# Routing weights from two fp32r products, x kept in DRAM meanwhile, steps from tile 40

## What is computed

```python
def peer_ffn(h, w_q, sub_keys, peer_u, peer_v):       # 8 heads, 128 x 128 experts, top 16
    q = einsum('td,de->te', xb, w_q)
    s = einsum('thpk,pnk->thpn', q, sub_keys)         # scores of two halves of a key
    s_top, i_top = top_k(s, 16)
    g_top, pos = top_k(sums of the two halves, 16)    # 16 experts (i, j) per head and token
    g = softmax(g_top)
    act = gelu(einsum('thk,td->thk', peer_u[expert], xb))
    return einsum('thk,thkd->td', g * act, peer_v[expert])
```

## Time and profile before

| | |
|---|---|
| median of 3 runs | 2617.55 us |
| the profiled execution's own time | 2617.07 us |
| its span (first to last instruction) | 2615.2 us |
| TensorE (PE) busy | 2562.4 us, 98% |
| VectorE (DVE) busy | 2056.7 us, 79% |
| ScalarE (ACT) busy | 1549.1 us, 59% |
| mean granted TensorE clock | 0.992 |

### The profile page before, as it was taken

One profiled execution on the slowest core, in us unless ns is written; L12 is line 12 of the kernel. 1 busy time (PEld: TensorE's weight loads), 2 busy tenths in 40 slices (PEclk: granted clock), 3 DMA queues, 4 the chain that ended last, 5 costly groups with the idle time before them and its releaser, 6 DMA issues.

```text
span 2615.2 us, 46815 instructions
## 1 busy us (share of the span) xinstructions
PE 2562.4 (98%) x16116; PEld 2305.1 (88%) x16116; DVE 2056.7 (79%) x4002; ACT 1549.1 (59%) x2687; POOL 321.2 (12%) x182
## 2 busy tenths in 40 slices
PE   6999999999999999999999999999999999999998
PEld 5779989999888888989989999888888888889887
DVE  6778978889888887679878888766666886688866
ACT  3455577766666666555577666665554555564543
POOL 3107700000000002717500000000000001100000
PEclk8999999999999999999999999999999999999999
DMA  6845574444788885424564444555556356643554
GB/s 228 285 151 173 187 248 151 145 141 148 259 291 289 292 281 163 170 95 166 203 225 146 146 145 146 201 193 201 192 192 207 106 166 203 202 149 131 182 192 137
DMA packets 138427, 492.42 MB, mean 188 GB/s; under 512 B 18704, under 2 KB 18792, under 8 KB 137984
## 3 DMA queue, kind: packets, MB, share of 16 engines
q1 hardware_dynamic: 135600, 481.90, 53.8%
q0 software_dynamic: 2640, 8.02, 1.0%
HBM read 488.79 MB, written 1.07 MB: 187 GB/s over the span
## 4 chain that ended last, share of the span: by engine, by line
PE 90%; DVE 6%; ACT 2%; DMA 1%; issue 1%; POOL 0%; SPq 0%; DVEq 0%; ACTq 0%
PE ps L236 70%; PE ps L242 7%; PE ps L1491 4%; PE ps L243 4%; DMA weight_ring<-in_stream 1%; DVE weight_split L271 1%; PE ps L2659 1%; PE ps L1455 1%; DVE hT_split L496 1%; ACT weight_split L262 0%; DVE hT_split L495 0%; DVE stat L621 0%; PE ps L450 0%; DVE x L618 0%; POOL weight_split L271 0%
## 5 line engine op out<-in xcount | busy, mean ns | idle before, releaser
L262 ACT ACTIVATE weight_split<-weight_ring 128x1024 fp32r<-128x1024 f32 x800 | 848.7, 1062 | 228.4 <-DMA weight_ring<-in_stream 139.2
L271 DVE TENSOR_TENSOR weight_split<-weight_ring,weight_split 128x1024 fp32r<-128x1024 f32 x684 | 829.5, 1221 | 135.1 <-ACT weight_split L262 131.7
L236 PE MATMUL ps<-hT_split,weight_split 128*128 128x256 f32 x7224 | 923.5, 286 | 4.2 <-POOL weight_split L271 2.3
L236 PE MATMUL ps<-weight_split,hidden_split 128*128 128x512 f32 x3948 | 911.3, 390 | 0.0
L236 PEld LDWEIGHTS ps<-hT_split,weight_split 128*128 128x128 f32 x7224 | 885.7, 193 | 10.8 <-issue 7.1
L236 PEld LDWEIGHTS ps<-weight_split,hidden_split 128*128 128x128 f32 x3948 | 736.2, 188 | 156.1 <-issue 1.0
L271 POOL TENSOR_TENSOR weight_split<-weight_ring,weight_split 128x1024 fp32r<-128x1024 f32 x116 | 282.2, 2438 | 123.0 <-ACT weight_split L262 122.8
L242 PE MATMUL ps<-hT_split,weight_split 128*128 128x512 f32 x816 | 291.4, 398 | 0.5 <-DVE hT_split L496 0.5
L1586 ACT ACTIVATE hidden_split<-arena 128x256 fp32r<-128x256 f32 (+1 forms) x256 | 175.4, 685 | 178.5 <-PE ps L236 178.1
L1758 DVE TENSOR_TENSOR hidden_split<-arena,hidden_split 128x256 fp32r<-128x256 f32 x256 | 163.8, 640 | 90.5 <-ACT hidden_split L1586 90.1
L243 PE MATMUL ps<-hT_split,weight_split 128*128 128x256 f32 x816 | 229.0, 281 | 0.0
(11 more groups left out here) (377 smaller groups left out, 1979.5 us busy)
## 6 DMA issues: line engine op xcount, KB each, us to landing
weight_ring<-in_stream SPq DMA_DIRECT2D x912, 512.0 KB, 3.4
arena<-gate_rows SPq DMA_DIRECT2D x3, 512.0 KB, 5.4
x<-in_x SPq DMA_DIRECT2D x1, 1024.0 KB, 5.1
arena<-mlstm_m_rows POOLq DMA_DIRECT2D x1, 1024.0 KB, 6.1
arena<-in_ln_mix_g POOLq DMA_DIRECT2D x2, 512.0 KB, 5.4
arena<-in_ln_mix_b POOLq DMA_DIRECT2D x2, 512.0 KB, 7.9
arena<-in_ln_ffn_g POOLq DMA_DIRECT2D x2, 512.0 KB, 4.8
arena<-in_ln_ffn_b POOLq DMA_DIRECT2D x2, 512.0 KB, 6.7
```

The source lines that it names most:

```text
L236: mm = pe.matmul(out_, stationary(s_part), moving(m_part), start=start and n == 0, stop=stop and n == 2, skip_group_check=True)
L262: act.activation(wsplit[:, n % SPLITS, HIGH, :], ring[:, slot(POS[n]), :], ACT.Copy).then_inc(high_ready, 1)
L271: eng.tensor_tensor(w[:, REST, :], ring[:, slot(POS[n]), :], w[:, HIGH, :].bitcast(fp32), ALU.subtract).then_inc(split_ready, 1)
```

## The change

- An expert's weight w is parted into its rounding to fp32r, h, and the ratio (w - h) / h (`weight_parts`, VectorE, once per layer ahead of the first step). `places_i` now holds h, in fp32r. A token takes two fp32r matmuls in place of one fp32 matmul, with the same stationary matrix: one with the ones of the second place, one with the ratio in their place. Their sum is w.
- VectorE makes the ones for all 4 tokens of a step (`places_j`), first in its pass; ScalarE multiplies them with the ratio, 4 activations with a scale per partition (`places_low`), which wait for VectorE. The distance and the Relu go.
- `pr_ohi` and the ratio's matrices lie where x is; x is written to DRAM at the start of the up stage and read back in the down stage, both by SyncE's queue. The places of the ones have two buffers, not three.
- STEP_AT: 64 steps over tiles 40 to 124, at a distance of 1.2 tiles at first and 1.5 at the end. Wide tiles are 30 to 39, no more 30 to 50; a step ahead of tile 51 weighs and keeps in the early part of `acts` too.

```diff
-("down0", "ssa", 56), ...  ("down1", "s", 64), ...
+("down0", "ssa", 8), ("down0_more", "ssa", 48), ...  ("down1", "s", 16), ("down1_more", "s", 48), ...
-STEP_AT = [j for j in range(52, 125) if (j - 52) % 8 != 7]
+STEP_AT = [40 + (1512 * q + 27 * q * q // 10) // 1260 for q in range(64)]
+WIDE_FROM = 30
...
+        with nc.sbuf_tensor("step_parts", [128, 2, 2, 4, 128], fp32r) as step_parts:
+            pass
         x = sbuf("x", [128, TB, D])
...
-        pr_ohi = edge_b.rearrange("p (n a i) -> p n a i", n=2, a=STEP)
-        pr_ohj = hidden[:].rearrange("p n a t -> p (n a t)").rearrange("p (n a i) -> p n a i", n=3, a=STEP)
+        pr_ohi, pr_ohj_low = step_parts[:, 0], step_parts[:, 1]
+        pr_ohj = hidden[:, 0:2].rearrange("p n a t -> p (n a t)").rearrange("p (n a i) -> p n a i", n=2, a=STEP)
+        pr_low, pr_high = hidden[:, 2, 0, :], hidden[:, 2, 1, :]
...
         def wide(j):
-            return 30 <= j < 51
+            return WIDE_FROM <= j < FIRST_STEP
...
                 for a in range(STEP):
-                    mm = pe.matmul(ps[:, q % 3, 128 * a:128 * a + 128], pr_ohi[:, q % 2, a, :], pr_ohj[:, q % 3, a, :].bitcast(fp32),
-                                   start=True, stop=True)
+                    weights = ps[:, q % 3, 128 * a:128 * a + 128]
+                    pe.matmul(weights, pr_ohi[:, q % 2, a, :], pr_ohj[:, q % 2, a, :], start=True, stop=False, skip_group_check=True)
+                    mm = pe.matmul(weights, pr_ohi[:, q % 2, a, :], pr_ohj_low[:, q % 2, a, :], start=False, stop=True, skip_group_check=True)
...
+            def places_low(q):
+                if q == 0:
+                    act.wait_ge(pr_low_r, l + 1)
+                    act.wait_ge(x_moved, 16 * (2 * l + 1))
+                act.wait_ge(pr_ohj_dve, STEPS * l + q + 1)
+                if q >= 2:
+                    act.wait_ge(pr_built, STEPS * l + q - 1)
+                for a in range(STEP):
+                    t = STEP * q + a
+                    step = act.activation(pr_ohj_low[:, q % 2, a, :], pr_ohj[:, q % 2, a, :].bitcast(fp32), ACT.Copy, scale=pr_low.bitcast(fp32)[:, t:t + 1])
+                step.then_inc(pr_ohj_act, 1)
...
             for j in range(128):
+                if j + 1 in STEP_AT:
+                    places_low(with_step(j + 1))
                 if j - 1 in STEP_AT:
                     keep(with_step(j - 1))
-                if j + 1 in STEP_AT:
-                    places_j(with_step(j + 1))
...
+            def weight_parts():
+                dve.wait_ge(pr_cols_out, 2 * (l + 1))
+                whole, high, inverse = pr_cols[:, 2, :], pr_high.bitcast(fp32), edge_b[:, 0:T]
+                after_dve(dve.tensor_copy(pr_high, whole))
+                after_dve(dve.tensor_tensor(whole, whole, high, ALU.subtract), dve.tensor_scalar(inverse, high, 1e-30, None, ALU.max))
+                after_dve(dve.reciprocal(inverse, inverse))
+                dve.tensor_tensor(pr_low, inverse, whole, ALU.mult).then_inc(pr_low_r, 1)
+                dve.wait_ge(pr_low_r, l + 1)
+                dve.wait_ge(x_moved, 16 * (2 * l + 1))
...
             for j in range(HEAD, 129):
+                if j + 1 in STEP_AT:
+                    if with_step(j + 1) == 0:
+                        weight_parts()
+                    places_j(with_step(j + 1))
                 if j - 1 in STEP_AT:
                     weigh(with_step(j - 1))
...
-                if j + 1 in STEP_AT:
-                    places_j(with_step(j + 1))
...
+            dve.wait_ge(x_moved, 16 * (2 * l + 2))
             residual_dve(2 * l + 1, 3 if l else 1, edge_b, td + 128, HY_T if l else SB_T, None if l else 2)
...
+            def x_out(l):
+                eng.wait_ge(x_ready, 2 * l + 1)
+                eng.dma_start(x_kept, x[:]).then_inc(x_moved, 16)
+
+            def x_back(l):
+                eng.wait_ge(pr_built, STEPS * (l + 1))
+                eng.dma_start(x[:], x_kept).then_inc(x_moved, 16)
+
+            beside = {"up0": lambda: x_out(0), "down0_more": lambda: x_back(0), "up1": lambda: x_out(1), "down1_more": lambda: x_back(1),
```

More of the change, by code:

```diff
@@ L1595, in keep @@
                 act.wait_ge(pr_routed, STEPS * l + q + 1)
[L1596 to L1600, removed]
-                for a in range(ACT_J):
-                    step = act.activation(pr_ohj[:, q % 3, a, :], iota[:], ACT.Abs, scale=-1.0, bias=pr_cols[:, 1, STEP * q + a:STEP * q + a + 1])
-                step.then_inc(pr_distance, 1)
-                act.wait_ge(pr_distance, STEPS * l + q + 1)
-                near = pr_ohj[:, q % 3, 0:ACT_J]
-                act.activation(near, near.bitcast(fp32), ACT.Relu, scale=-1.0, bias=1.0).then_inc(pr_ohj_act, 1)
+                at, tokens = STEP_AT[q], slice(STEP * q, STEP * q + STEP)
+                if at < EARLY:
+                    act.activation(acts_early[:, tokens, at:], step_weights(q)[:, :, at:EARLY], ACT.Copy)
+                late = max(at, EARLY)
+                act.activation(acts_late[:, tokens, late - EARLY:], step_weights(q)[:, :, late:], ACT.Copy).then_inc(pr_kept, 1)
+            def places_low(q):
[9 more added lines that the diff above has]
+                step.then_inc(pr_ohj_act, 1)
             def exps():
@@ L1739, in places_i, with places_j @@
             def places_i(q):
+                for a in range(STEP):
+                    t = STEP * q + a
+                    step = dve.tensor_scalar(pr_ohi[:, q % 2, a, :], iota[:], pr_cols[:, 0, t:t + 1], pr_high.bitcast(fp32)[:, t:t + 1], ALU.is_equal, ALU.mult)
+                step.then_inc(pr_ohi_r, 1)
+            def places_j(q):
                 if q >= 2:
                     dve.wait_ge(pr_built, STEPS * l + q - 1)
-                for a in range(STEP):
-                    t = STEP * q + a
-                    step = dve.tensor_scalar(pr_ohi[:, q % 2, a, :], iota[:], pr_cols[:, 0, t:t + 1], pr_cols[:, 2, t:t + 1], ALU.is_equal, ALU.mult)
-                step.then_inc(pr_ohi_r, 1)
-            def places_j(q):
-                if q >= 3:
-                    dve.wait_ge(pr_built, STEPS * l + q - 2)
-                dve.tensor_tensor(pr_ohj[:, q % 3, ACT_J:], iotas(STEP - ACT_J), chosen(1, STEP * q + ACT_J, STEP * q + STEP), ALU.is_equal).then_inc(pr_ohj_dve, 1)
+                dve.tensor_tensor(pr_ohj[:, q % 2], iotas(STEP), chosen(1, STEP * q, STEP * q + STEP), ALU.is_equal).then_inc(pr_ohj_dve, 1)
             def down_rest(j, i=0):
@@ L3025, in refill @@
                 eng.dma_start(ring[:, slot(pos), :], src).then_inc(tile_full[slot(pos)], 16)
-            beside = {"up0_late": lambda: gate_row_out_sp(1), "down0_late": gate_down0_sp, "sb": lambda: gate_row_out_sp(2), "sb_v": gate_sb_sp,
+            def x_out(l):
[5 more added lines that the diff above has]
+            beside = {"up0": lambda: x_out(0), "down0_more": lambda: x_back(0), "up1": lambda: x_out(1), "down1_more": lambda: x_back(1),
+                      "up0_late": lambda: gate_row_out_sp(1), "down0_late": gate_down0_sp, "sb": lambda: gate_row_out_sp(2), "sb_v": gate_sb_sp,
                       "up1_late": lambda: gate_row_out_sp(3), "down1_end": gate_peer1_sp}
```

28 lines of the change are left out of this document (15 added, 13 removed), and 4 rows, old and new, of the table SEGMENTS.

## The result

The changed kernel takes 2625.7 us (median of 7 runs, 2624.51 to 2627.25). The kernel before takes 2615.58 us in 7 runs beside them. The ratio is 1.0036, with a 95% interval of 1.0025 to 1.0048: 10.1 us slower. The forecast was 2625.8 us. The agreement to 0.1 us is luck: the profiled execution of before, on which the sum stood, is 1.5 us above the median of 7, and the terms of the sum are short by 1.3.

What follows compares the result with a forecast made beforehand. TensorE, busy 98% of the span, was taken as the bound; steps 0.9, narrow tiles 1.1, holes ahead of the first step 6.2 and x back 0.6 sum to +8.8 us on 2617.07, 2625.8 us, range 2577 to 2640.

Steps and rivals of the forecast that it cites:

- The step on TensorE: In the 128 steps, 8 weight loads before and after set the pace: 0.893 us a step against 0.886, +0.9 us.
- both rivals on the step: On TensorE: columns set the pace, 0.53 us a step (chance 0.20); fp32r slow below 256 columns, 1.77 us (0.06).
- Narrow tiles: In the up stages, 22 wide tiles turn narrow, 2.88 us each on TensorE against 2.83: +1.1 us.
- Ahead of the first step: Between tiles 39 and 44, weight_parts on VectorE makes TensorE wait: 3.1 us a layer, +6.2 us.
- Beside the steps afterwards: From tile 44 on, VectorE's and ScalarE's mean work stays under TensorE's: 0 us.
- x out and back: Transfers of x: out in the up stage 0, back in down0 +0.6 us, in the second layer 0.
- The base and the sum: Whole kernel: terms of +8.8 us on the profiled execution's 2617.07 us give 2625.8 us.

Runs made afterwards that it cites:

- e2: The changed kernel with the second product of each token moving 64 columns in place of 128: 2624.1 us.
- e3: The changed kernel with the second product of each token using 64 of the 128 stationary columns: 2596.7 us.
- e6: The changed kernel with weight_parts in four pieces in passes 32 to 38: 2621.2 us; U, the second layer's up stage over the kernel before, +1.4 us.
- e7: The changed kernel with the reciprocal of weight_parts left out: 2620.9 us in one execution.
- e4: The kernel before with only x's transfers to DRAM and back added, at the change's places in SyncE's queue: 2617.0 us.
- e5: The changed kernel with x read back in the first layer behind the adaLN rows, not at tile 16 of down0: 2623.5 us.
- e9: The kernel before with one fp32r product per token, the weight's rest left out, and steps from tile 44: 2559.8 us.
- e10: The changed kernel with weight_parts in four passes, x read back late and the second product's matrices in bf16: 2601.2 us.
- e8: The changed kernel with weight_parts in four passes and x read back late: 2618.1 us.

## Why the prediction was right, step by step

- **The step on TensorE.** Right in the bound and nearly in size. I predicted 0.893 us from the distance of two loads of a single-column matmul; 8 x 0.112 is 0.896, so this was a slip, and +1.3 us was meant where +0.9 stands. Measured are 0.895 against 0.886, and +0.013 us from step to step with the tile beside it, 1.7 us for 128 steps. Before and after are 8 loads. What I did not see is that the kernel before has fp32 records with a load of 8 columns (90 ns) that stand 0.11 us apart too with 128 moving columns, and 0.22 with 256 (L1094, L1093). The changed kernel itself refutes both rivals on the step: its matmuls start 0.11 us apart, not 0.067 and not over 0.2. e2 and e3 show that it is the load.
- **Narrow tiles.** A wide tile is 0.353 us a pair as before, 2.83 us, and a narrow one 2.88; 22 tiles are 1.1 to 1.2 us. No run measures this alone, but the terms close: 64 times 0.013 and 11 times 0.054 are 1.4 us a layer, and e6's U, with no hole left, is 1.4.
- **Ahead of the first step.** Predicted 3.1 us a layer in holes of 1.7, 0.9 and 0.5; the distances show 1.2, 0.6 and 0.6 above the usual one, and the move of weight_parts in e6 gives back 2.5. So this term is 5.0 us for 6.2. The order, ScalarE's scaled copies as what came last and the reciprocal's 1.75 us were as drawn. The size was off in the small operations: the chain took 3.2 us for 3.5 (its first cast 0.29 for 0.44) and began 0.3 us sooner, and the four scaled copies took 1.28 for 1.38. The handing on was better described by my working than by my later expectation of e7.
- **Beside the steps afterwards.** Zero, as predicted: from tile 44 on no hole up to the last step, VectorE busy for 241 of 278 us.
- **x out and back.** Out 0, as e4's up stages show. Back was the term that was mis-sized most: 0.6 predicted, against 1.8 by e4's median, 2 to 3 by e5's and 4.0 in the profiled execution's down0. I took the cover of one tile (2.9 us) against the transfer's own time at the 281 GB/s of that stretch (3.7). The transfer took 8.1 us to land among the weight tiles, and the stage's DMA is 83% busy. That it therefore cannot win its cover back, so that small waits later on show as well, is my reading of the later holes at 733 to 849 us; no run tests it.
- **The base and the sum.** 2617.07 stood 1.5 us above the median of before. So the move was 10.1 us where the sum had 8.8 on that base. Measured term by term it is 1.7 for the steps, 1.2 for the narrow tiles, 5.0 for the holes and 2.2 for what is left, the way back. The mechanisms were right; that the forecast came out only 0.1 us off is because three wrong sizes and a high base nearly cancel.

## What to carry to other kernels

Count weight loads beside products and columns. Here, with 128 columns to a matmul, the other type of product gained nothing, as it needs a second load of the same matrix: 8 loads a step, 0.111 us apart before and 0.112 after. What gained was half the loads (2.2% in e9, without the weight's low part), one of 64 columns in each pair (0.7% in e3, without half of the low part), or one in bf16 (0.6% in e10). Preparation that stands once in front of the first step belongs passes earlier, an operation at a time, with a look at the slow ones (the reciprocal, 1.75 us; the move gave back 2.5 us a layer in e6). And look at how busy the DMA is where a transfer is put in: at 83% in down0 this one cost some 2 us for the 0.6 that I had from its cover, and nothing in the second layer, where no adaLN rows are in the stream (62% busy from 1637 to 1990 us, the transfer among them).

## What the runs showed of the hardware

- In the changed kernel's steps, fp32r loads of 128 columns start 0.112 us apart between matmuls that move 128 columns, and the same when every second one moves 64 (pair 0.22 us in e2). With 64 stationary columns in every second one the pair takes 0.17 us (e3, both matmuls moving 128 columns).
- Each fp32 matmul of the steps stands in the trace of before as two matmul records and two loads (1024 each for 512, L1491), and so do those of L1093 and L1094 (16 for 8). With 8 stationary columns the two records start 0.22 us apart at 256 moving columns (L1093) and 0.11 at 128 (L1094); with 128 stationary columns and a single moving one they start 0.112 us apart.
- A bf16 load of a 128x128 matrix lasts 96 ns (e10), one of fp32r 192 in the changed kernel and 201 in e10; a pair of one bf16 and one fp32r matmul takes 0.19 us (e10).
- VectorE's reciprocal of 256 columns took 1.75 us on 128 partitions (L1752, changed kernel), against 0.29 to 0.43 for the operations around it.
- GpSimd's copy of 128x512 from fp32r to bf16 took 1.5 us in the median (0.6 to 2.7) beside VectorE, and VectorE's 128x512 comparison was 5% longer beside it (e10 against e8).
- A transfer of 1 MB issued among weight tiles took 8.1 us to land in down0 of the changed kernel, where the DMA share around it was 0.88 (712 to 740 us), and 6.4 in down1, where no adaLN rows are in the stream.
